# A joined four-block kernel: one scan with resets per head, squares by ScalarE, and new places for small steps

## The reference

```python
x = x + rms_norm(even_mixer(rms_norm(x)))   # "even": retention + stick-breaking attention
x = x + rms_norm(odd_mixer(rms_norm(x)))    # "odd", the second mixer: HGRN2 + RG-LRU
x = diff attention + conformer conv; swiglu # "diff", "ffn0"
x = S5 state space + latent attention; swiglu   # "ssm", "ffn1"

def hgrn2(q, f_logit, i, lb):               # 4 heads of 128
    log_f = logaddexp(log(lb), log1p(-lb) + log_sigmoid(f_logit))
    k = (1.0 - lb) * sigmoid(-f_logit)
    b = cumsum(log_f) within a chunk; decays exp(b_t - b_s) between q and k
def rg_lru(x, ...):                         # 512 channels
    log_a = -8 * r * softplus(-lam);  a = exp(log_a)
    mult = sqrt(-expm1(2 * log_a));  mult[0] = 1
    h = scan(a, mult * ig * x)
```

## Time and profile before

| | |
|---|---|
| time, median of 3 (range) | 2041.15 us (2040.47 to 2041.37) |
| the profiled execution | 2041.19 us, its span 2039.4 us |
| granted TensorE clock, mean | 0.934 |
| busy: PE / weight loads / DVE / ACT / POOL | 88% / 66% / 47% / 36% / 45% |
| HBM | 136.5 MB read, 68 GB/s over the span |
| stages, roughly | even to 340, odd to 665, diff to 950, ffn0 to 1335, ssm to 1645, ffn1 to 2039 |

### The profile page before, as it was taken

One profiled execution on the slowest core, in us unless ns is written; L12 is line 12 of the kernel. 1 busy time (PEld: TensorE's weight loads), 2 busy tenths in 40 slices (PEclk: granted clock), 3 DMA queues, 4 the chain that ended last, 5 costly groups with the idle time before them and its releaser, 6 DMA issues.

```text
span 2039.4 us, 19949 instructions
## 1 busy us (share of the span) xinstructions
PE 1795.7 (88%) x7412; PEld 1350.4 (66%) x7412; DVE 960.8 (47%) x1483; ACT 738.5 (36%) x1207; POOL 926.9 (45%) x1100
## 2 busy tenths in 40 slices
PE   5999978988778888688999999978777889999996
PEld 3776556666665676456788888755444568888885
DVE  1043435675543699636321313655655554123244
ACT  4264554354344322454332222342222443322232
POOL 3433124465653444024565656467123336556563
PEclk9999999988988899898999999997778899999998
DMA  4311012122111122012232332211000112233231
GB/s 169 93 63 63 31 42 82 62 63 72 42 32 52 62 73 73 11 42 73 85 102 93 98 99 94 77 60 49 11 11 21 42 63 93 94 100 96 93 97 69
DMA packets 39553, 139.89 MB, mean 69 GB/s; under 512 B 4512, under 2 KB 4640, under 8 KB 39328
## 3 DMA queue, kind: packets, MB, share of 16 engines
q1 hardware_dynamic: 39456, 138.61, 21.3%
HBM read 136.50 MB, written 2.10 MB: 68 GB/s over the span
## 4 chain that ended last, share of the span: by engine, by line
PE 72%; DVE 17%; ACT 7%; issue 2%; POOL 1%; DMA 0%; SPq 0%; DVEq 0%; ACTq 0%; POOLq 0%
PE ps L576 18%; PE ps L577 18%; PE ps L578 18%; DVE ps L1734 3%; PE ps L605 2%; PE ps L589 1%; PE ps L2146 1%; PE ps L591 1%; PE ps L590 1%; PE ps L841 1%; PE ps L2123 1%; POOL wl L2631 1%; PE ps L1150 1%; PE ps L2137 1%; DVE arena L679 1%
## 5 line engine op out<-in xcount | busy, mean ns | idle before, releaser
L2631 POOL TENSOR_TENSOR wl<-raw,wh 128x256 fp32r<-128x256 f32 x988 | 802.8, 843 | 975.8 <-ACT wh L630 975.4
L576 PE MATMUL ps<-hh,wh 128*128 128x512 f32 x1204 | 518.3, 431 | 72.8 <-DVE hl L693 46.0
L577 PE MATMUL ps<-hl,wh 128*128 128x512 f32 x1204 | 479.1, 398 | 0.0
L578 PE MATMUL ps<-hh,wl 128*128 128x512 f32 x1204 | 478.7, 398 | 0.0
L630 ACT ACTIVATE wh<-raw 128x1024 fp32r<-128x1024 f32 x247 | 261.0, 1057 | 559.6 <-PE ps L578 511.2
L576 PEld LDWEIGHTS ps<-hh,wh 128*128 128x128 f32 x1204 | 232.9, 193 | 150.7 <-DVE hl L693 52.1
L576 PE MATMUL ps<-mh,wh 128*128 128x512 f32 x632 | 267.8, 424 | 48.5 <-DVE ml L937 7.8
L577 PEld LDWEIGHTS ps<-hl,wh 128*128 128x128 f32 x1204 | 232.7, 193 | 62.0 <-issue 17.7
L578 PEld LDWEIGHTS ps<-hh,wl 128*128 128x128 f32 x1204 | 232.0, 193 | 50.6
L577 PE MATMUL ps<-ml,wh 128*128 128x512 f32 x632 | 254.0, 402 | 0.0
L578 PE MATMUL ps<-mh,wl 128*128 128x512 f32 x632 | 253.8, 402 | 0.0
(11 more groups left out here) (464 smaller groups left out, 2223.6 us busy)
## 6 DMA issues: line engine op xcount, KB each, us to landing
raw<-in_w SPq DMA_DIRECT2D x247, 512.0 KB, 3.5
x<-in_x SPq DMA_DIRECT2D x8, 256.0 KB, 6.9
out<-x SPq DMA_DIRECT2D x8, 256.0 KB, 2.0
arena<-in_rope SPq DMA_DIRECT2D x3, 512.0 KB, 4.9
arena<-in_dec SPq DMA_DIRECT2D x1, 1024.0 KB, 11.3
mats<-in_mats SPq DMA_DIRECT2D x1, 576.0 KB, 7.9
arena<-in_lw SPq DMA_DIRECT2D x1, 512.0 KB, 3.8
arena<-in_levels SPq DMA_DIRECT2D x1, 448.0 KB, 4.5
```

What stands on the lines that cost most here:

```text
L576: e.matmul(ps[b][:], a, xh, start=first, stop=False)
L577: e.matmul(ps[b][:], a, xl, start=False, stop=False)
L578: e.matmul(ps[b][:], l, xh, start=False, stop=final).then_inc(pe.sem, pe.up(*step))
L2631: e.tensor_tensor(wl[:, n % NHL, cut(i, 2)], raw[:, n % NRAW, cut(i, 2)], wh[:, n % NHL, cut(i, 2)].bitcast(F32), SUB).then_inc(split.sem, ...
```

## The change

The lists, and with them the order of every engine, change in five places; the rest follows from that.

1. Start: weight slots 0, 1, 2 are issued after tiles 0, 1 and 3 of x, the constants after tile 1. ACT loads its table first, works on tile 0 of x, and rounds slots 0, 1, 2 ahead of tiles 1, 2, 3; it copies the constants ahead of tile 4. PE waits for these copies only at its last `sq`.
2. Second mixer: the groups `gl`, `gg`, `hq`, `hf` turn through four banks instead of two. The square of a is an exponential with scale 2 on ACT. The factor 1 - lb of k is the bias log(1 - lb) of the exponential that makes k. One scan of 512 for each head, with a mask that is 0 at the start of each chunk, does the four. The last subtraction of `le` is a step of its own, `lf`, a place or more later.
3. ffn0: the pieces `ds` follow the evictions of pairs 0, 1, 2, 3, 5, 7, 8, 9. ACT therefore loads the sigmoid's table after the sines.
4. ssm: `s1`, `s2`, `s3` are cut into `s1`, `s1b`, `s2`, `s2b`, `s2c`, `s3`, `s3b`, `s3c`, of one or two DVE operations each; the list of scans, now 81 steps instead of 41, is spread over the same matmuls, so that its few last steps (`s4`, `z1` to `z4`) lie closer to the end.

```diff
@@ -192,7 +192,7 @@
     out += merge(groups([("gl", j) for j in range(4)], 8, "e", "gm"), lru)
-    late = [("la", j) for j in range(4)] + [("lq",)] + [("le", j) for j in range(4)]
+    late = [("la", j) for j in range(4)] + [("lq",), ("le", 0), ("le", 1), ("lf", 0), ("le", 2), ("lf", 1), ("le", 3), ("lf", 2), ("lf", 3)]
@@ -248,7 +248,7 @@
 
-def steps_ffn(*besides):
+def steps_ffn(**besides):
@@ -262,12 +262,13 @@
             out += mul
-            pend = [("e1", f), ("e2", f), ("e3", f)]
+            pend = [("e1", f), ("e2", f), ("e3", f)] + besides.get(f"f{f}", [])
+            if f == 0:
+                out += besides.get("first", [])
...
             out += groups([("d", third, d) for d in range(KT)], b - a, "de")
-    last = closing(THIRDS[2][1] - THIRDS[2][0])
-    return out + merge(last[:-24], besides) + last[-24:] if besides else out + last
+    return out + closing(THIRDS[2][1] - THIRDS[2][0])
@@ -307,7 +308,8 @@
     for i in range(0, 8, 2):
-        scan += [("s1", i), ("s2", i), ("s1", i + 1), ("s3", i), ("s2", i + 1), ("s3", i + 1)]
+        scan += [("s1", i), ("s1b", i), ("s2", i), ("s2b", i), ("s1", i + 1), ("s1b", i + 1), ("s2c", i), ("s3", i), ("s3b", i)]
+        scan += [("s3c", i), ("s2", i + 1), ("s2b", i + 1), ("s2c", i + 1), ("s3", i + 1), ("s3b", i + 1), ("s3c", i + 1)]
@@ -317,7 +319,8 @@
 
-STEPS = {"even": steps_even(), "odd": steps_odd(), "diff": steps_diff(), "ffn0": steps_ffn(*[("ds", n) for n in range(8)]),
+STEPS = {"even": steps_even(), "odd": steps_odd(), "diff": steps_diff(), "ffn0": steps_ffn(first=[("ds", 0)], f1=[("ds", 1)], f2=[("ds", 2)], f3=[("ds", 3)], f5=[("ds", 4)], f7=[("ds", 5)],
+                                                                         f8=[("ds", 6)], f9=[("ds", 7)]),
@@ -390,7 +393,7 @@
     "even": {"sq": (0, 1, 2, 3), "sk": (0, 1, 2, 3), "sg": (0, 1), "rq": (0, 1), "rg": (0,), "p": (0, 1), "o": (0, 1, 2, 3)},
-    "odd": {"lx": (0, 1, 2, 3), "gl": (0, 1), "gg": (0, 1), "hq": (0, 1), "hf": (0, 1), "p": (0, 1), "o": (0, 1, 2, 3)},
+    "odd": {"lx": (0, 1, 2, 3), "gl": (0, 1, 2, 3), "gg": (0, 1, 2, 3), "hq": (0, 1, 2, 3), "hf": (0, 1, 2, 3), "p": (0, 1), "o": (0, 1, 2, 3)},
@@ -600,7 +603,8 @@
                         e.wait_ge(s_mats, 16)
-                        e.wait_ge(consts.sem, consts[EXACT[-1]])
+                if stage == "even" and k == KT - 1:
+                    e.wait_ge(consts.sem, consts[EXACT[-1]])
@@ -978,10 +982,15 @@
             e.wait_ge(s_vec, 16)
-            e.preload_act_table_set(EXP_LN)
...
                 kind = step[0]
+                if kind == "hi" and 1 <= step[1] <= NHL:
+                    round_slot(e, step[1] - 1)
+                if step == ("hi", NHL + 1):
+                    e.wait_ge(s_mats, 16)
+                    for name in EXACT:
+                        e.activation(R(name), M(name), ACT.Copy).then_inc(consts.sem, consts.up(name))
@@ -1078,11 +1087,12 @@
         GL, lx = cv(4, T), cv(4, T + PAD)
-        o_sig, a_sq = [cv(T), cv(T)], cv(T)
+        o_sig, resets = [cv(T), cv(T)], cv(T)
...
         a4 = lx[:, :, PAD:]
+        a_sq = [nrm[:, 4, :], nrm[:, 5, :]]
@@ -1226,6 +1236,10 @@
                     e.tensor_tensor(ca, c1, al, SUB).then_inc(dve.sem, dve.up("ca"))
+                elif kind == "bd":
+                    e.memset(resets, 1.0).then_inc(dve.sem, dve.up("ones"))
+                    e.wait_ge(dve.sem, dve["ones"])
+                    e.memset(fours(resets)[:, :, 0:1], 0.0).then_inc(dve.sem, dve.up("resets"))
@@ -1270,12 +1284,8 @@
                     j = step[1]
-                    m = a_sq
-                    if j:
-                        e.wait_ge(dve.sem, dve["one_less", j - 1])
-                    e.wait_ge(act.sem, act["a", j])
-                    e.tensor_tensor(m, a4[:, j, :], a4[:, j, :], MUL).then_inc(dve.sem, dve.up("a_squared", j))
-                    e.wait_ge(dve.sem, dve.n)
+                    m = a_sq[j % 2]
+                    e.wait_ge(act.sem, act["a_squared", j])
@@ -1291,6 +1301,8 @@
                     e.tensor_tensor(rr[:, j, :], rr[:, j, :], GL[:, j, :], MUL).then_inc(dve.sem, dve.up("mix", 4 + j))
+                elif kind == "lf":
+                    j = step[1]
@@ -1306,17 +1318,13 @@
                     j = step[1][1]
-                    a, ls, f = nrm[:, 2 + j % 2, :], nrm[:, 4 + j % 2, :], k4[:, j, :]
-                    e.wait_ge(act.sem, act["other", j])
-                    e.tensor_scalar(f, f, om[:, j:j + 1], None, MUL).then_inc(dve.sem, dve.up("k", j))
+                    a, ls = nrm[:, 2 + j % 2, :], nrm[:, 4 + j % 2, :]
...
                     e.wait_ge(dve.sem, dve.n)
-                    for i in range(4):
-                        e.tensor_tensor_scan(c4[:, j, cut(i)], M("ones"), ls[:, cut(i)], 0.0, MUL, ADD).then_inc(
-                            dve.sem, dve.up("summed", j, i))
+                    e.tensor_tensor_scan(c4[:, j, :], resets, ls, 0.0, MUL, ADD).then_inc(dve.sem, dve.up("summed", j, 3))
@@ -1423,7 +1431,10 @@
                     e.wait_ge(act.sem, act["tanh", j])
+                    if j >= 2:
+                        e.wait_ge(dve.sem, dve["one_less", j - 2])
                     e.activation(a4[:, j, :], rr[:, j, :], ACT.Exp).then_inc(act.sem, act.up("a", j))
+                    e.activation(a_sq[j % 2], rr[:, j, :], ACT.Exp, scale=2.0).then_inc(act.sem, act.up("a_squared", j))
@@ -1448,9 +1459,9 @@
                     e.wait_ge(dve.sem, dve["log_other", j])
-                    e.activation(f, f, ACT.Exp).then_inc(act.sem, act.up("other", j))
...
                         e.wait_ge(dve.sem, dve["ca"])
+                    e.activation(f, f, ACT.Exp, scale=1.0, bias=c1[:, j:j + 1]).then_inc(act.sem, act.up("k", j))
@@ -2355,18 +2366,29 @@
                     e.tensor_tensor(vim, ps[7][:], cosT, MUL).then_inc(dve.sem, dve.up("s_b", i))
+                elif kind == "s1b":
+                    i = step[1]
+                    vre, vim, w5, w6 = lane_of(i)
+                    cosT, sinT = angle_at[i]
...
                     vre, vim, w5, w6 = lane_of(i)
-                    mg = mag[:, i:i + 1].to_broadcast([128, T])
...
                     e.tensor_tensor(vim, vim, w6, SUB).then_inc(dve.sem, dve.up("s_im", i))
+                elif kind == "s2b":
+                    i = step[1]
+                    vre, vim, w5, w6 = lane_of(i)
+                    mg = mag[:, i:i + 1].to_broadcast([128, T])
...
                     e.tensor_tensor_scan(w5, mg, vre, 0.0, MUL, ADD).then_inc(dve.sem, dve.up("scan_re", i))
+                elif kind == "s2c":
+                    i = step[1]
+                    vre, vim, w5, w6 = lane_of(i)
+                    mg = mag[:, i:i + 1].to_broadcast([128, T])
@@ -2377,9 +2399,16 @@
                     e.tensor_tensor(vim, w6, cosT, MUL).then_inc(dve.sem, dve.up("s_f", i))
+                elif kind == "s3b":
+                    i = step[1]
+                    vre, vim, w5, w6 = lane_of(i)
+                    cosT, sinT = angle_at[i]
...
                     e.tensor_tensor(w5, w5, sinT, MUL).then_inc(dve.sem, dve.up("s_h", i))
+                elif kind == "s3c":
+                    i = step[1]
+                    vre, vim, w5, w6 = lane_of(i)
@@ -2434,7 +2463,7 @@
                 e.activation(tabs, a6, ACT.Sin, scale=6.283185).then_inc(act.sem, act.up("tabs"))
-                e.preload_act_table_set(EXP_LN)
+                e.preload_act_table_set(SIGMOID)
@@ -2611,12 +2640,8 @@
         def scalar_program(e):
+            e.preload_act_table_set(EXP_LN)
             e.wait_ge(consts.sem, consts["set", 2])
-            for n in range(NHL):
-                round_slot(e, n)
-            e.wait_ge(s_mats, 16)
-            for name in EXACT:
-                e.activation(R(name), M(name), ACT.Copy).then_inc(consts.sem, consts.up(name))
@@ -2657,9 +2682,9 @@
                 e.dma_start(x[:, k, :], io["x"][:, k, :]).then_inc(s_x[k], 16)
-                if k in (1, 3, 7):
-                    load_slot(e, k // 3)
-                if k == 3:
+                if k in (0, 1, 3):
+                    load_slot(e, (k + 1) // 2)
+                if k == 1:
```

## The result

The changed kernel takes 2011.35 us (median; 2009.26 to 2011.61) against 2041.26 (2040.47 to 2042.83) for the kernel before, a ratio of 0.985 with a 95% interval of 0.9833 to 0.9867. Its profiled execution took 2009.26 with a span of 2007.5. The forecast was 2010.2 in a range of 1997 to 2021. One execution of the kernel before, in the rounds of the first experiments, took 2185 us at a mean clock of 0.805 and is left out of every comparison.

What follows compares the result with a forecast made beforehand. TensorE (72% of the last chain) bounds the kernel, so only its earlier start or shorter waits count. Opening -10.0, second mixer -9.6, feed-forward -7.4, ssm -4 sum to -31: from 2041.19 to 2010.2 us, range 1997 to 2021.

Steps and rivals of the forecast that it cites:

- Root and recurrences: Second mixer: roots end 0.8 us earlier and fewer waits and subtractions save 2.8, so ACT's next chain starts 3.5 earlier.
- behind it DVE has one scan of 1.23 instead of four ... -2.1: Second mixer, decays: behind the last head's softplus, one scan replaces four on DVE, worth -2.1 us.
- Until 477 PE only gets to its wait earlier: Second mixer, four banks: no gain before 477 us, since DVE ends last there.
- those wait for ACT and DVE instead: Second mixer, four banks: PE's 5.61 us gate wait goes, but level matmuls wait instead; -2 taken of 0 to -5.6.
- The memory set: Second mixer: one MEMSET of 128x512 for the resets, in front of the convolution, costs 0.4 us, bounds 0 to 0.7.
- No wait above 3.5 for line 2499's successor: Sign in ssm: no PE wait for an exponential of the scores longer than 3.5 us.
- the tail term: End of ssm: last scan step and GELU come later, so the low half of z starts +4.9 us later, PE idle.
- (A): Rival in ssm: the pieces don't help and the tail stays, +5 us instead of -4, total 2019; chance 0.15.
- (D): Rival in ssm: finer pieces put one operation more before each of 24 row units, slower, total 2048; chance 0.02.
- (E): Rival for the whole kernel: effects are there, but other things hold the stages and nothing shows; chance 0.03.
- (B): Rival: gains add up further, banks release their 5.6 us and ssm pieces 11.5 less 1, total 2000; chance 0.15.
- (C): Rival in the opening: a slot, constants or x piece 4 hold PE, half of 10 us lost, total 2015; chance 0.07.

Runs made afterwards that it cites:

- the first experiments: Four kernels, each the kernel before with one part of the change; ratios: opening 0.9924, second mixer 0.9943, "ffn0" 0.9976, "ssm" 0.9955.
- lru_only: Kernel before with ACT's square of a and the later subtraction, but four scans, multiply and two banks kept; by-token wait ends 140.5 us into the stage, against 141.8.
- four_scans: Changed kernel with four scans of 128 back in place of one of 512; wait before the by-token product ends 138.0 us into the stage, against 135.4.
- early5: Kernel before with one matmul left out of each of the 22 gate groups of "ffn0"; 2035.16 us, against 2044.99 beside it.
- late5: Kernel before with one matmul more in each of the 22 gate groups of "ffn0"; 2044.42 us, against 2044.99 beside it.
- only_banks2: Kernel before with four banks instead of two in the second mixer and nothing else; 2037.74 us, against 2044.99 beside it.

## Why the prediction was right, and where it was not

The total came within 0.1%, but partly because two errors cancelled. Forecast and measured, profile against profile: opening -10.0 and -8.8; second mixer -9.6 and -6.9; "ffn0" -7.4 and -7.2; "ssm" -4 and -9.1; the rest 0 and 0.

**Opening.** The mechanism held step by step: slot 0 rounded at 6.96 (forecast 6.9). The term that was mis-sized is the split, 2.75 us a slot from a row in which DVE had nothing to do; beside DVE's low halves it is 6.46 / 2 = 3.2, and PE starts at 11.46 instead of 10.9. The 0.7 lost at the fourth slot behind the decay table was named as a cost of 0 to 1.5 and counted at nothing. These two, 0.6 and 0.7, are the whole difference between -10.0 and -8.8: PE's busy time in this stage is 292.9 in the one profile and 292.8 in the other. That the clock was equal is luck, as the unchanged stage moves by 4.7 us between profiles.

**Second mixer.** Root and recurrences: -3.5 forecast for the start of the decays; -3.9 measured in lru_only, -3.3 in the changed kernel (435.00, 108.1 into the stage). Behind it -4.5 was forecast and 3.0 came. The step that failed is "behind it DVE has one scan of 1.23 instead of four ... -2.1". The row used, 3.30, is of the first head beside POOL; the last head, the one in front of PE's wait, took 1.37 already and now takes 1.63. In place of it the scans of the *earlier* heads count, as four_scans shows with 2.6: with them DVE has no gap from 441.78 to its last scan, where the changed kernel has 2.1 us of gaps. In all -6.4 at that wait instead of -8.0. The banks alone gave 0.5 of the 2.0 behind that wait: "those wait for ACT and DVE instead" was right, its size was not. "Until 477 PE only gets to its wait earlier" was wrong once the decays start sooner: in lru_only DVE waits 2.01 for PE there. The memory set took 0.48, where 0.4 was taken, and made PE's wait for the convolution 0.69 longer, the upper bound, as it stands between two DVE operations for which PE waits.

**Feed-forward.** From the last low half of the mix to the last eviction there are now 1308.69 - 1273.33 = 35.4 us, against 35.1 in "ffn1", and no gap of PE in the gate groups:

```profile
1273.33 0.69 DVE L1955 TENSOR_TENSOR ml<-arena,mh 128x512 fp32r<-128x512 f32 x1 [0.70 <-ACT mh L1986]
...
1308.69 0.69 DVE L707 TENSOR_TENSOR arena<-ps,arena 128x512 f32<-128x512 f32 x1 [2.26 <-PE ps L581]
```

**ssm.** "No wait above 3.5 for line 2499's successor" failed: the longest is 7.4, at 1411.79, and one of 4.23 stands at 1479.03. But the waits for it fell by 29.1 - 23.7 = 5.4. A new wait before the GLU product was forecast with 5 and came with 2.7 + 0.6: the tail term was too large by 1.7. With -6.0 of standing still where -4 stood, the mechanism was right; the other 3.1 are the clock. That the total came out so close is luck in this: these 3.1 and the 2 of waits make up for what the other terms lacked.

**Rivals.** (A), (D) and (E) are out by the stage lengths. (B) was half right: the pieces did bring more than -4, but in standing still 6.0 of its 10.5; the banks did not. (C) came with 0.7 of its 5 us. What is open: what makes an unchanged "ssm" take 303 or 311 us. Its start doesn't. Whether the 3.1 us of clock belong to the one execution of the kernel before or to its code is open too. For the second speaks that early5, late5 and only_banks2 lie 5 to 7 us lower beside it than their stages explain, with one run each; a kernel's own executions would have to be profiled several times.

## What to carry to other kernels

Take a duration from the instance that stands on the path and from the moment at which it will run, not from the first row of its kind: the same four scans took 3.3 and 1.37 us in one trace. And before a stage's difference between two profiles is called a gain, split it into PE's standing still and PE's busy time with equal matmul counts; the second part is the clock, and another execution need not have it. Parts that are timed alone can claim more than the whole has: 41 us here against 31, while their standing still adds up to within 2.4 us.

## What the runs showed of the hardware

- PE's time for equal work in a stage with many short waits differs between profiles of kernels with the same code there by up to 8 us in 310 (PE busy for 242.0 to 250.4 us with 882 or 883 matmuls, at a mean clock of 0.85 and 0.82), while its standing still stays within 60.0 to 62.2.
- DVE's scans pay per instruction for POOL at work: 0.34 us to 0.83 for a scan of 128 columns (1.37 and 3.30 for four), 1.22 to 1.65 for one of 512. POOL pays too: 3.2 us a slot instead of 2.75.
- An operation of DVE with an input in PSUM pays nothing: 0.68 to 0.69 us in 44 instances (line 1933), where one with both inputs in SBUF takes 0.68 to 1.25 (line 1937).
- A MEMSET of 128x512 takes 0.48 us.
